# Six slices of a dense SwiGLU with seven half products in place of eight, on one Trainium2 core

## What is computed

```
def swiglu(h, w_gate, w_up, w_down):
    return (jax.nn.silu(h @ w_gate) * (h @ w_up)) @ w_down
hn = rms_norm(h, ffn_norm[0])                      # (256, 1024)
h = h + swiglu(hn, dense_w_gate[0], dense_w_up[0], dense_w_down[0])   # 1024 x 3584, 1024 x 3584, 3584 x 1024
```

## Time and profile before

| what | value |
|---|---|
| median of three runs | 1490.58 us (1490.28 to 1490.66) |
| profiled execution, first to last instruction (its span) | 1489.1 us |
| mean granted TensorE clock | 0.998 of full speed |
| PE busy | 1477.0 us (99%) |
| DVE / ACT / POOL busy | 1189.9 (80%) / 947.9 (64%) / 116.2 us (8%) |
| DMA moved | 445.60 MB, mean 299 GB/s |
| dense part on PE (first matmul at line 1073 to last at line 1110) | 193.4 to 431.4 us |

### The profile page before, as it was taken

The page is one execution under the profiler, slowest core; times in us unless marked ns, Lnnn a source line. Parts: engine busy times, 40 slices in busy tenths (PEclk is TensorE's granted clock), DMA queues, the critical chain, the costliest instruction groups (busy, mean ns, idle before and its releaser), DMA issues.

```text
span 1489.1 us, 20171 instructions
## 1 busy us (share of the span) xinstructions
PE 1477.0 (99%) x7900; PEld 1234.6 (83%) x7900; DVE 1189.9 (80%) x1056; ACT 947.9 (64%) x852; POOL 116.2 (8%) x77
## 2 busy tenths in 40 slices
PE   9999999999999999999999999999999999999998
PEld 7999988888887788888888888888888888888886
DVE  5977775444478699889889889898898988988985
ACT  4554544434465676777677777677777677767773
POOL 0470110000013000000000000000000000000000
PEclk9999999999999999999999999999999999999999
DMA  6331885555414299999999999999999999999990
GB/s 227 114 115 58 307 320 181 173 209 183 169 58 156 99 396 393 396 383 393 397 382 394 393 369 386 381 371 381 383 380 372 389 380 363 391 383 359 395 362 30
DMA packets 186696, 445.60 MB, mean 299 GB/s; under 512 B 5399, under 2 KB 5680, under 8 KB 186635
## 3 DMA queue, kind: packets, MB, share of 16 engines
q1 hardware_dynamic: 182208, 430.12, 77.7%
q0 software_dynamic: 3936, 14.20, 3.3%
q10 hardware_dynamic: 490, 0.42, 0.1%
HBM read 437.89 MB, written 7.89 MB: 299 GB/s over the span
## 4 chain that ended last, share of the span: by engine, by line
PE 96%; DVE 2%; DMA 1%; ACT 0%; POOL 0%; issue 0%; SPq 0%; DVEq 0%; ACTq 0%
PE bank L1482 14%; PE bank L1484 14%; PE bank L1483 14%; PE bank L1467 7%; PE bank L1469 7%; PE bank L1468 7%; PE bank L698 4%; PE bank L1145 3%; PE bank L1144 3%; PE bank L1143 3%; PE bank L785 2%; PE bank L789 2%; PE bank L790 2%; PE bank L791 2%; PE bank L1132 1%; PE bank L1130 1%
## 5 line engine op out<-in xcount | busy, mean ns | idle before, releaser
L2625 DVE TENSOR_TENSOR ring_r<-ring,buf_r 128x2048 fp32r<-128x2048 f32 x336 | 751.2, 2284 | 28.0 <-ACT buf_r L1926 28.0
L1926 ACT ACTIVATE buf_r<-ring 128x2048 fp32r<-128x2048 f32 x336 | 629.4, 1914 | 52.5 <-PE bank L1469 43.3
L1482 PE MATMUL bank<-ring_r,buf_r 128*128 128x512 f32 x896 | 354.5, 396 | 0.3 <-DVE buf_r L2745 0.3
L1484 PE MATMUL bank<-buf_r,buf_r 128*128 128x512 f32 x896 | 349.6, 390 | 0.0
L1483 PE MATMUL bank<-buf_r,buf_r 128*128 128x512 f32 x896 | 349.0, 389 | 0.0
L1484 PEld LDWEIGHTS bank<-buf_r,buf_r 128*128 128x128 f32 x896 | 168.0, 188 | 36.0
L1482 PEld LDWEIGHTS bank<-ring_r,buf_r 128*128 128x128 f32 x896 | 168.4, 188 | 33.6 <-DVE buf_r L2745 0.4
L1483 PEld LDWEIGHTS bank<-buf_r,buf_r 128*128 128x128 f32 x896 | 168.5, 188 | 33.4
L1467 PE MATMUL bank<-ring_r,buf_r 128*128 128x512 f32 x440 | 172.8, 393 | 0.1
L1469 PE MATMUL bank<-buf_r,buf_r 128*128 128x512 f32 x440 | 171.5, 390 | 0.0
L1468 PE MATMUL bank<-buf_r,buf_r 128*128 128x512 f32 x440 | 171.2, 389 | 0.0
(11 more groups left out here) (378 smaller groups left out, 1867.1 us busy)
## 6 DMA issues: line engine op xcount, KB each, us to landing
ring<-in_moe_w_gate SPq DMA_DIRECT2D x56, 2048.0 KB, 10.0
ring<-in_moe_w_up SPq DMA_DIRECT2D x56, 2048.0 KB, 10.4
ring<-in_moe_w_down SPq DMA_DIRECT2D x56, 2048.0 KB, 10.4
ring<-in_a_w_in SPq DMA_DIRECT2D x8, 2048.0 KB, 8.5
ring<-in_dense_w_gate SPq DMA_DIRECT2D x7, 2048.0 KB, 7.8
ring<-in_dense_w_up SPq DMA_DIRECT2D x7, 2048.0 KB, 7.9
ring<-in_dense_w_down SPq DMA_DIRECT2D x7, 2048.0 KB, 8.0
ring<-in_a_w_out SPq DMA_DIRECT2D x2, 2048.0 KB, 10.9
```

Source lines behind the costliest of these rows:

```text
L1482: pe.matmul(o, xh, low[:, c], start=k == 0, stop=False)
L1484: ins = pe.matmul(o, xh, high[:, c], start=False, stop=k == KT - 1)
L1926: act.activation(HB[m % NHB], half_words(m, U_MOE), ACT.Copy).then_inc(m_wh, 1)
L2625: dve.tensor_tensor(half_low(m, U_MOE), half_words(m, U_MOE), HB[m % NHB], ALU.subtract).then_inc(m_wl, 1)
```

## The change

Slice 0 stays as it was. Slices 1 to 6 form three pairs. Each pair's gate, and each pair's up, is one group ("quad", six in all): the activation is cut in 2 token tiles x 2 halves of the model width, the weight in 2 halves of the width x 2 slices, and the product of the 2 x 2 blocks is made with seven half products in the Strassen-Winograd form in place of eight. A half product is 12 matmuls (4 blocks x 3) and uses one 1 MB block of weights. Four of a quad's seven blocks are sums of weight quarters ("t"), three are plain quarters ("w"). The stage becomes 60 blocks of 1 MB: 4 of slice 0 with 24 matmuls each, 42 of quads with 12 each, and 14 halves of down with 24 each.

- The sums of weights are made in DRAM, in `weight_sums`, by DMAs on POOL's queue: for each pair 8 copies of 1 MB (`sums_first`), then 4 (`sums_second`), 2 (`sums_third`) and 2 (`sums_fourth`) accumulating DMAs of 1 MB. Each of the four steps waits on POOL until the DMAs of the step before have landed.
- SP loads blocks of 1 MB into six slots (twelve half slots); a "t" block waits until all 16 DMAs of its pair have landed.
- Sums of activations are made by DVE (`mixed_rows`) and split once. The pieces of a quad's result are put together by ACT (`first_part`, `fifth_part`), DVE (`sixth_part`, `last_piece`, `side_piece`, `fourth_piece`) and POOL (`both_parts`, `quad_hidden`).
- The gate's seventh product ("t", 3) stands between the two halves of a down slice; the up's directly behind its six.
- Small tables (`RBW`, `RBT`) move to another buffer and are loaded later; some semaphores are merged.

```
+PAIRS = (NSL - 1) // 2
+QUADS = 2 * PAIRS
+SUMS = 16
+def dense_blocks():
+    out = [("w", kind, 0, half) for kind in ("gate", "up") for half in range(2)]
+    for qd in range(QUADS):
+        p, kind = quad_pair(qd), quad_kind(qd)
+        j = 2 * p - 1
+        out += [("w", kind, j, 0), ("t", qd, 1), ("t", qd, 0), ("w", kind, j, 1), ("t", qd, 2),
+                ("w", kind, j + 1, 1)]
+        if kind == "gate":
+            out += [("d", max(0, 2 * p - 3), 0), ("t", qd, 3), ("d", max(0, 2 * p - 3), 1)]
+        else:
+            out += [("t", qd, 3)]
+            out += [("d", 2 * p - 2, half) for half in range(2) if p > 1]
+    return out + [("d", j, half) for j in (NSL - 2, NSL - 1) for half in range(2)]
...
         @block.sync
+            def dense_loads():
+                for m in range(NB):
+                    if m < 4:
+                        sp.wait_ge(proj_mm, 16)
+                    elif m < 6:
+                        sp.wait_ge(vn_mm, 2)
+                    elif m < 8:
+                        sp.wait_ge(o_mm, 4)
+                    elif m < 12:
+                        sp.wait_ge(wo_mm, 4)
+                    elif m < NB - 2:
+                        sp.wait_ge(d_used, m - 11)
+                    else:
+                        sp.wait_ge(d_used, quad_at(QUADS - 1) + 6)
+                    if BLOCKS[m][0] == "t":
+                        sp.wait_ge(sums_done, 16 * SUMS * quad_pair(BLOCKS[m][1]))
+                    sp.dma_start(block_dst(m), block_src(m)).then_inc(slot_full[block_place(m)[0]], 16)
...
         @block.gpsimd
+            def sums_first(p):
+                j = 2 * p - 1
+                if p > 1:
+                    pool.wait_ge(sums_done, 16 * SUMS * (p - 1))
+                for qd in (2 * p - 2, 2 * p - 1):
+                    kind = quad_kind(qd)
+                    for r, src in ((0, quarter(kind, j, 0)), (2, quarter(kind, j + 1, 0)), (1, quarter(kind, j, 0)),
+                                   (3, quarter(kind, j, 1))):
+                        pool.dma_start(sums(qd, r), src).then_inc(sums_done, 16)
+            def sums_second(p):
+                j = 2 * p - 1
+                pool.wait_ge(sums_done, 16 * (SUMS * (p - 1) + 8))
+                for qd in (2 * p - 2, 2 * p - 1):
+                    kind = quad_kind(qd)
+                    for r, src in ((2, quarter(kind, j + 1, 1)), (0, quarter(kind, j + 1, 0))):
+                        pool.dma_start(sums(qd, r), src, accum_op=ALU.add, max_dma_last_dim=2048).then_inc(sums_done, 16)
+            def sums_third(p):
+                pool.wait_ge(sums_done, 16 * (SUMS * (p - 1) + 12))
+                for qd in (2 * p - 2, 2 * p - 1):
+                    pool.dma_start(sums(qd, 1), sums(qd, 2), accum_op=ALU.add, max_dma_last_dim=2048).then_inc(sums_done, 16)
+            def sums_fourth(p):
+                pool.wait_ge(sums_done, 16 * (SUMS * (p - 1) + 14))
+                for qd in (2 * p - 2, 2 * p - 1):
+                    pool.dma_start(sums(qd, 3), sums(qd, 1), accum_op=ALU.add, max_dma_last_dim=2048).then_inc(sums_done, 16)
             pool.wait_ge(lev_in, 16)
             pool.wait_ge(cst_rest, 16)
+            pool.wait_ge(proj_mm, 2)
+            sums_first(1)
...
             for lv in range(3, NLEV - 1):
                 for g in range(4):
                     level_mask(lv, g)
+                if lv == 3:
+                    sums_second(1)
                 if lv == 4:
...
+                    sums_third(1)
+            sums_fourth(1)
             for t in range(TT):
                 power(sm(264 + t * HEADS, HEADS))
+                if t == 0:
+                    sums_first(2)
+            sums_second(2)
             power(sm(192, 1))
             pool.wait_ge(pow_out, powers[0])
...
             power(sm(193, 1))
+            sums_third(2)
+            sums_fourth(2)
...
+            def both_parts(qd):
+                out = (QPR if qd % 2 else QSG)[:, 1, 1, :].rearrange("p (k q) -> p k q", q=P)
+                pool.wait_ge(first_out, 2 * qd + 2)
+                pool.tensor_tensor(out, out, FIRSTP, ALU.add).then_inc(quad_p, 1)
+            def quad_hidden(p):
+                qd = 2 * p - 1
+                for i, (sl, t) in enumerate(((1, 1), (1, 0), (0, 1))):
+                    pool.wait_ge(part_v, 4 * qd + 2 + i)
+                    pool.wait_ge(sg_ready, 2 * TT + 4 * (p - 1) + 2 + i)
+                    pool.tensor_tensor(QPR[:, sl, t, :], QPR[:, sl, t, :], QSG[:, sl, t, :], ALU.mult
+                                       ).then_inc(quad_p, 1)
+            for qd in range(QUADS):
+                both_parts(qd)
+                if qd == 0:
+                    sums_first(3)
+                if qd == 1:
+                    quad_hidden(1)
+                    sums_second(3)
+                    sums_third(3)
+                    sums_fourth(3)
+                elif qd % 2 == 1:
+                    quad_hidden(quad_pair(qd))
...
         PE
+            def product(m, bank, of, start=False):
+                pe.wait_ge(d_wl, m + 1)
+                low, high = block_low(m), block_high(m)
+                for k in range(4):
+                    c = slice(k * FS, (k + 1) * FS)
+                    ah, al = of(k)
+                    pe.matmul(bk[bank][:, :], ah, low[:, c], start=start and k == 0, stop=False, skip_group_check=not start)
+                    pe.matmul(bk[bank][:, :], al, high[:, c], start=False, stop=False, skip_group_check=not start)
+                    ins = pe.matmul(bk[bank][:, :], ah, high[:, c], start=False, stop=k == 3, skip_group_check=not start)
+                ins.then_inc(d_used, 1)
...
         DVE
+            def last_piece(qd):
+                o = quad_out(qd)[:, 1, 1, :]
+                dve.wait_ge(quad_p, pool_part(qd))
+                dve.wait_ge(d_used, quad_at(qd) + 5)
+                dve.scalar_tensor_tensor(out=o, in0=bk[B_BANK][:, :], scalar=-1.0, in1=o, op0=ALU.mult, op1=ALU.subtract
+                                         ).then_inc(part_v, 1)
...
+                for qd in range(QUADS):
+                    s = quad_at(qd)
+                    if m == s + 5:
+                        sixth_part(qd)
+                    if m == s + 7:
+                        if qd % 2 == 1:
+                            first_hidden(qd)
+                        last_piece(qd)
+                    if m == s + 9:
+                        side_piece(qd)
+                    if m == fourth_at(qd) + 3:
+                        fourth_piece(qd)
+                if m < NB:
+                    dense_low(m)
```

More of the change, by code:

```diff
@@ new lines, in fourth_product, with down_blocks @@
+            def fourth_product(qd):
+                pe.wait_ge(part_v, 4 * qd + 2)
+                product(fourth_at(qd), B_BANK, rows_of(1, 1))
+            def down_blocks(j, halves=range(2)):
+                for half in halves:
+                    m = BLOCKS.index(("d", j, half))
+                    pe.wait_ge(d_wl, m + 1)
+                    if half == 0:
+                        pe.wait_ge(ht_ready, 2 * j + 2)
+                    for t in range(TT):
+                        ins = down(m, t)
+                    ins.then_inc(d_used, 1)
+                    hidden_turns(m)
```

434 lines of the change are left out of this document (286 added, 148 removed).

## The result

The changed kernel takes 1618.49 us (median of four runs, 1618.2 to 1623.35), the kernel before on the same chip 1490.55 us: 1.0867 times as long, with a 95% interval of 1.0852 to 1.0882. That is 128 us slower, and 40 us above the upper end of the predicted range.

What follows compares the result with a forecast made beforehand. PE, busy 99% of the span, was taken as the bound. -16.3 + 2 + 2 + 17 + 0 + 32 = +37 us gave 1527.6 us; range 1478 to 1578 us.

Steps and rivals of the forecast that it cites:

- What is taken away: On PE, six quads need 84 matmuls in place of 96, 72 fewer in all: -16.3 us.
- What DVE, ACT and POOL get: 18 more blocks to split, in long rows of half products: costed at nothing, 0 to +5 us for three rows.
- What the DMA engines get: the price of adding: On the DMA engines, an accumulating DMA of 1 MB costs between 2.7 us, like a copy, and 5.4 us.
- Pair 1, copies: Copies from 29 us share the engines with the load of 42.8 us: +2 us, 0 to +5.
- Pair 1, second round: Adds issued at 86 us, POOL must go on with level 5 at 103.2 us: +2 us, 0 to +8.
- Pair 2, the norm: POOL's wait for eight copies in `sums_second(2)` delays the norm's `power(sm(192, 1))`: +17 us, +5 to +24.
- Pair 2, later rounds: POOL reaches `both_parts(0)` after the later rounds, about when DVE wants it: 0, up to +10 us.
- Pair 3: Rounds two to four on POOL between `quad_hidden(1)` and `both_parts(2)` make the latter late: +32 us, +19 to +64.
- The room: DMA engines idle 197 us up to 415 us; needs of 179 or 244 us overdraw the usable part by 19 or 62.
- Rival B: Same waits at the full price of adding: +60 to +100 us, 1551 to 1589 us, chance 0.20.
- Rival A: Copies and sums hide beside the loads: 1474 us, up to 1487 with small waits, chance 0.22.
- Rival C: DVE bounds the long rows of half products: at most +5 us, 1479 without late sums; chance within A's and the forecast's.

Runs made afterwards that it cites:

- e2: Changed kernel without the 48 DMAs of sums and their waits, splits of the last four turned blocks put where PE turns them: 1485.36 us.
- e1: Changed kernel without the 48 DMAs of sums and their waits, plain weight quarters loaded in place of sums: 1501.82 us.
- e8: e2 with the splits of pair 1's last two turns one block earlier in the order of ACT and DVE: 1485.39 us.
- e4: Changed kernel with the 24 accumulating DMAs made plain copies, all 48 DMAs and POOL's waits kept: 1566.62 us.
- e10: Changed kernel, all sums, transfers started as early as data allow, rounds rearranged, own count for pair 2, last four turns in PE's order: 1571.56 us.
- e9: Changed kernel with all eight adds of a pair in one round, sources all quarters of the inputs: 1615.65 us.
- e7: Changed kernel, all sums, pair 1's copies spread, pair 2's behind the norm, later rounds of pairs 2 and 3 moved back, last turns reordered: 1600.63 us.
- e3: Changed kernel with only the 24 copies made and waited for, the 24 accumulating DMAs left out: 1531.36 us.

## Why the prediction was wrong

The sign was right, and so was the mechanism for pair 3; the size was not: +37 us was forecast, 128 came. Two steps failed. The adding DMAs were priced near the lower end, like copies, and the transfers at 53 us in all, where 116.7 came; and the pieces and splits of DVE, ACT and POOL were put at nothing, where 27.6 came. Of the 91 us between, 27.6 are pieces and last splits (11.1 + 16.5, costed at nothing), and 63.7 are copies and sums (29.5 + 35.3 + 51.9 = 116.7 in place of 53). By places on the time line: 25.7 us of delay for pair 1 and 17.6 up to the norm, both with what the clock cost; then PE's waits alone, 11.3 + 5.4 for pair 2's later rounds and 57.6 for pair 3. That these add up to 117.6 is partly chance: the later ones leave out the clock.

- **What is taken away.** 72 matmuls are gone, as said. But PE is busy for 1487.8 us where e2, with the same instructions, needs 1462.1: 25.7 us more, of which 6.0 are there in e1 already, behind the last splits. After waits the clock granted is the lower of its two levels, 1.2 GHz: it is 0.50 from 390 to 410 us, in the middle of the wait of 35.64 us, and 0.61 in the stretch in which PE starts again:

```profile
382.00:418.00 36.00, 0.36 (x2) 0.23 (x2) 3.23 (x3) 2.43 (x2) 5.38 (x5) 0.57 1.08 304
418.00:422.00 4.00, 4.00 (x12) 3.17 (x13) 4.00 (x4) 0.85 (x2) 0.00 (x0) 0.61 1.13 208
422.00:432.00 10.00, 10.00 (x46) 8.29 (x45) 8.46 (x5) 7.32 (x6) 0.00 (x0) 1.00 0.59 151
```

  The prediction counted every wait at its own length alone. No run fills such a wait with other matmuls, so this is a reading of rows and not tested by itself.
- **What DVE, ACT and POOL get: costed at nothing, with 0 to +5.** This failed twice. DVE is full in a row of half products; e2 and e8 show 8.0 us of waits, above my +5. The turns want their splits at once, and DVE is busy without a gap from 262 to 284 us, so it has no lead when they come. And the last four splits, 16.5 us, were not in the sum at all: I had put the order of the splits with the edits that cost nothing and did not follow `high_place` for blocks 56 to 59. ACT and DVE take their programs in order, so these are to be read line by line at the end of a loop, where a rule made for its middle changes.
- **What the DMA engines get: the price of adding.** Between the ends of 2.7 and 5.4 us the forecast leaned to the lower one; measured are 5.04 us. The row that I had, the scatter-add with 301 in place of 387 GB/s, had told it: nearly twice its bytes. With 5.04 us the need is 42 x 2.7 + 24 x 5.04 = 234 us against 182 us of room, overdrawn by 52. The changed kernel doesn't even use that room: its engines stand at 0.63 and 0.84 up to 200 us, so that 37 + 16 = 53 us of the 197 stay idle and some 90 are overdrawn. The changed kernel against e4 shows the term: +51.9 us.
- **Pair 1, copies: +2, 0 to +5.** PE waits 11.44 us. I took two halves for the two queues. The profile's part 3 for 44 to 56 us, the time in which the load issued at 44.2 us should have landed, shows another share (queue, packets, MB, share):

```profile
q0 software_dynamic: 785, 3.03, 79.3%
```

  3.03 of 3.90 MB went to POOL's queue; the load took 23.6 us to land. From 182 to 212 us POOL's queue had 7.25 of 11.60 MB. In e10, with four copies in place of eight in the way, the wait is gone.
- **Pair 1, second round: +2, 0 to +8.** PE waits 6.86 us at 134 us, for the masks of level 5 as forecast: `sums_third(1)`, which waits for the second round ahead of them, held POOL for 10.87 us until 129.38. That is 28 us after the first issue at 101.36, where the upper end allowed 21.7; a load of 2 MB shared the engines. With the clock after both waits, `a_w_out` is issued at 177.43 in place of 151.69: 25.7 us for the two terms together, in place of 4.
- **Pair 2, the norm: +17, +5 to +24.** Right in size by luck: `power(sm(192, 1))` is 43.3 us late, of which 25.7 are there already, and the rest is 17.6. The wait that I described, `sums_second(2)` for the copies ahead of this power, held nothing: its input came behind it, and PE waited 0.31 us for the rows. The 17.6 us came by what I had put "beside this", the late `a_w_out` (PE's waits of 2.15 and 7.12 us), and by the eighth copy, which held the power of the mixer's own norm (PE's waits of 1.80 and 1.63 us behind it), which nothing in the trace of before showed.
- **Pair 2, later rounds: 0, up to +10.** 11.29 us at 294, behind `both_parts(0)` as described, and 5.40 more at 329, where ACT had waited 9.87 us for a block of sums: above the upper end together.
- **Pair 3: +32, +19 to +64.** 35.64 us for the wait that I described, near the value. With the 22 us of waits just before it, where ACT waits for blocks that landed late (10.23, 8.02 and 3.70 us at 347 to 368), it is 57.6, inside the range. Those I had left out, though the sentence that loads would be late stood among the things that would prove me wrong.
- **The room.** 197 us of idle engines hold as a count of the trace before, and the sentence that the sums can't be free was the sound part. But the overdraft is the least that the transfers cost: 19 to 62 us by the forecast, and some 90 with the room that stayed idle, of 116.7. I added up waits place by place and so lost what was not at a place that I knew. Rival B, the full price of adding, comes nearest: 1551 to 1589, and 27.6 us of pieces and last splits (11.1 + 16.5) on top give 1579 to 1617, just under what was measured.
- **Rival A** is out: POOL waits for `weight_sums` on the chain. **Rival C** was true, and larger than allowed, but shows only without sums.

No version found beats the kernel before, if it makes its sums: the fastest is e10 at 1.055. Without any sum and with the order mended the form gives 1485.4 us, 0.33% less than before, so that is what sums at no price could be worth here. Sums made on an engine from blocks already in the ring were not tried.

## What to carry to other kernels

Count a resource that will be full as a budget over the whole stretch: what the change asks of it, less what is idle before, is the least it costs. Collisions come on top: here 24 copies that fitted with ease cost 29.5 us. The order of the queues gave back 34 us, for an earlier start and better places together, and nothing was gained when POOL's waits went. A product saved on PE that asks for a transfer more is worth it only where the DMA engines have room; here 16.3 us of matmuls stood against 42 copies and loads and 24 adds. And take the sums out first when such a change disappoints: two runs without them showed that 27.6 of the 144 us lost (128 and the 16.3 that were saved) lay elsewhere.

## What was not expected of the hardware

- A queue can hold POOL itself: at the eighth copy of pair 2 for 31.29 us, in e9 at the eighth add for 41.54 us, in e7 at the fourth add for 28.50 us. It is no matter of a fixed number: the same eight copies went in within 5.0 us in e3 and e4, and pair 3's eight within 5.0 us at 307.03 in the changed kernel itself. What decides it is open.
- An adding DMA of 1 MB keeps POOL itself longer than a copy: four issues took from 101.36 to 105.6 us, the same four as copies in e4 from 99.87 to 102.4 us.
- Two queues don't share evenly: POOL's got 78% of the bytes from 44 to 56 us and 62% from 182 to 212 us. In the second stretch the packets are nearly even, 1873 of POOL's and 2159 of SP's, but POOL's hold 3.9 KB and SP's 2.0 KB.
